# Eight W-high matmuls and then eight W-low ones in a chunk, in place of two and two

## The reference

```
for l in range(2):
    hn = rmsnorm(x, norm_mix[l])
    y  = even_mixer(hn, w_in, ..., w_out)  or  odd_mixer(hn, w_in, ..., w_out)
    x  = x + y
    h  = rmsnorm(x, norm_ffn[l])
    u  = causal_dwconv(h @ w_up, conv_w, conv_b)
    gate, val = split(u, 2)
    x  = x + (gelu(gate) * val) @ w_down
```

## Time and profile before

| | us |
|---|---|
| median of three runs | 2254.8 |
| the profiled execution's own time | 2255.13 |
| its span, first to last instruction | 2253.3 |
| TensorE busy (matmul) | 2245.3 (100%) |
| weight loads busy | 1954.4 (87%) |
| VectorE busy | 1543.9 (69%) |
| ScalarE busy | 1160.2 (51%) |
| mean granted TensorE clock | 1.000 |

### The profile page before, as it was taken

How to read it: one execution, slowest core, us unless ns; L and a number is a source line. 1 busy time by engine, 2 the same in 40 slices (tenths; PEclk the granted TensorE clock), 3 DMA queues, 4 the chain that set the end, 5 groups by cost and what they waited for, 6 DMA issues and landing times.

```text
span 2253.3 us, 34392 instructions
## 1 busy us (share of the span) xinstructions
PE 2245.3 (100%) x12726; PEld 1954.4 (87%) x12726; DVE 1543.9 (69%) x1753; ACT 1160.2 (51%) x1342; POOL 7.2 (0%) x17
## 2 busy tenths in 40 slices
PE   9999999999999999999999999999999999999999
PEld 8888888888888888888888888888888888888888
DVE  7886776777777777554577777667777777774444
ACT  6654355555555555444355555555555555553333
POOL 0000000000000000000000000000000000000000
PEclk9999999999999999999999999999999999999999
DMA  7555555666666656555665554556666666566664
GB/s 272 182 178 165 191 177 186 181 193 191 182 188 188 201 177 192 190 182 192 200 211 164 173 178 157 169 185 183 191 192 184 187 187 201 179 190 203 198 189 144
DMA packets 216387, 420.92 MB, mean 187 GB/s; under 512 B 13062, under 2 KB 13590, under 8 KB 216177
## 3 DMA queue, kind: packets, MB, share of 16 engines
q1 hardware_dynamic: 214416, 413.59, 58.8%
q0 software_dynamic: 1456, 5.65, 0.7%
q10 hardware_dynamic: 432, 0.56, 0.1%
HBM read 417.62 MB, written 2.12 MB: 186 GB/s over the span
## 4 chain that ended last, share of the span: by engine, by line
PE 99%; DVE 0%; DMA 0%; ACT 0%; issue 0%; ACTq 0%; DVEq 0%
PE ps L664 61%; PE ps L668 30%; PE ps L706 2%; PE ps L707 2%; PE ps L705 2%; PE ps L744 0%; PE ps L790 0%; PE ps L802 0%; PE ps L726 0%; DMA x_res<-x_t 0%; PE ps L745 0%; PE ps L738 0%; PE ps L801 0%; DVE aq L951 0%; PE ps L762 0%; ACT cross L377 0%
## 5 line engine op out<-in xcount | busy, mean ns | idle before, releaser
L943 DVE TENSOR_TENSOR w_lo<-raw,w_hi 128x1024 fp32r<-128x1024 f32 x783 | 948.5, 1223 | 497.3 <-ACT w_hi L369 477.5
L664 PE MATMUL ps<-xs,w_hi 128*128 128x512 f32 x3968 | 1248.3, 396 | 3.7 <-DVE w_lo L1379 3.4
L369 ACT ACTIVATE w_hi<-raw 128x1024 fp32r<-128x1024 f32 x783 | 811.3, 1055 | 560.1 <-PE ps L668 510.7
L668 PEld LDWEIGHTS ps<-xs,w_lo 128*128 128x128 f32 x3968 | 745.4, 188 | 176.1
L668 PE MATMUL ps<-xs,w_lo 128*128 128x256 f32 x3968 | 779.5, 278 | 0.0
L664 PEld LDWEIGHTS ps<-xs,w_hi 128*128 128x128 f32 x3968 | 605.0, 189 | 6.1 <-DVE xs L992 3.5
L664 PE MATMUL ps<-act,w_hi 128*128 128x512 f32 (+1 forms) x1912 | 600.7, 395 | 0.0
L668 PEld LDWEIGHTS ps<-act,w_lo 128*128 128x128 f32 x1912 | 359.2, 188 | 84.9
L668 PE MATMUL ps<-act,w_lo 128*128 128x256 f32 (+1 forms) x1912 | 375.6, 278 | 0.0
L664 PEld LDWEIGHTS ps<-act,w_hi 128*128 128x128 f32 x1912 | 291.1, 189 | 0.4 <-DVE av L968 0.4
L380 ACT ACTIVATE cross<-ps 128x1024 f32<-128x1024 f32 x72 | 74.0, 1027 | 119.5 <-PE ps L668 119.1
(11 more groups left out here) (186 smaller groups left out, 865.0 us busy)
## 6 DMA issues: line engine op xcount, KB each, us to landing
raw<-w_up SPq DMA_DIRECT2D x352, 512.0 KB, 3.7
raw<-w_in SPq DMA_DIRECT2D x191, 512.0 KB, 3.8
raw<-w_down SPq DMA_DIRECT2D x176, 512.0 KB, 4.6
raw<-w_out SPq DMA_DIRECT2D x64, 512.0 KB, 4.6
bias<-bias_line POOLq DMA_DIRECT2D x1, 2048.0 KB, 9.6
x_res<-x_t SPq DMA_DIRECT2D x3, 512.0 KB, 7.7
out_t<-x_res POOLq DMA_DIRECT2D x3, 512.0 KB, 3.1
gates_w<-w_gates POOLq DMA_DIRECT2D x1, 1024.0 KB, 5.4
```

The source lines that it names most:

```text
L369: act_f(w_hi[:, s, :, :], raw[:, s, :, :], ACT.Copy).then_inc(hi_ready, 1)
L664: return mm(ps[:, 4 * group + m, :], w_hi[:, s, u, m * P:(m + 1) * P], rhs, start=first and u == 0, stop=False)
L668: return mm(ps[:, 4 * group + m, 0:S], w_lo[:, s, u, m * P:(m + 1) * P], rhs[:, 0:S], start=False, stop=last and u == CT - 1)
L943: tt(w_lo[:, s, :, :], raw[:, s, :, :], w_hi[:, s, :, :].bitcast(F32), ALU.subtract).then_inc(lo_ready, 1)
```

## The change

Both K-tiles' moving operands are formed first. Then come the eight matmuls with W_hi (K-tile 0: output tiles 0 to 3, K-tile 1: output tiles 0 to 3), and then the eight with W_lo in the same order. The wait for the second half of a drained group stays ahead of the first matmul of output tile 2, which is now the third of the chunk, where it was the fifth. The first chunk's second wait stays ahead of the first matmul of K-tile 1, now the fifth, where it was the ninth. `chunk_values`, `last_chunk` and every other engine's program are unchanged.

```diff
+            rhs = [src[:, bass.ds(kt + u, 1), :, :].rearrange("p t a s -> p (t a s)") for u in range(CT)]
             for u in range(CT):
                 if tile_wait is not None and u == 1:
                     pe.wait_ge(lo_ready, 1)
-                rhs = src[:, bass.ds(kt + u, 1), :, :].rearrange("p t a s -> p (t a s)")
-
-                def hi(m):
-                    return mm(ps[:, 4 * group + m, :], w_hi[:, s, u, m * P:(m + 1) * P], rhs,
-                              start=first and u == 0, stop=False)
-
-                def lo(m):
-                    return mm(ps[:, 4 * group + m, 0:S], w_lo[:, s, u, m * P:(m + 1) * P], rhs[:, 0:S],
-                              start=False, stop=last and u == CT - 1)
-
-                for m in range(0, BT, 2):
+                for m in range(BT):
                     if drained is not None and (u, m) == (0, BT // 2):
 
                         pe.wait_ge(acc_drained, drained)
-                    hi(m)
-                    hi(m + 1)
-                    lo(m)
-                    ins = lo(m + 1)
+                    mm(ps[:, 4 * group + m, :], w_hi[:, s, u, m * P:(m + 1) * P], rhs[u], start=first and u == 0, stop=False)
+            for u in range(CT):
+                for m in range(BT):
+                    ins = mm(ps[:, 4 * group + m, 0:S], w_lo[:, s, u, m * P:(m + 1) * P], rhs[u][:, 0:S],
+                             start=False, stop=last and u == CT - 1)
             ins.then_inc(chunk_used, 1)
```

## The result

Eleven runs of the changed kernel have a median of 2261.03 us (2259.99 to 2262.69), eleven of the kernel before 2255.15 (2254.23 to 2256.15). The ratio is 1.0025, with a 95% interval of 1.0018 to 1.0033: slower by 5.9 us, 0.25%. The profiled execution of the changed kernel took 2261.78 us, 6.65 more than that of before; its span is 2260.0 us, 6.7 more. Of experiment 10's six runs one took 3200.78 us at a mean granted clock of 0.654; it is left out of that experiment's median and ratio.

The account below looks back on a forecast made before the run. TensorE's matmul pace was taken to bound the kernel. 2255.13 us + 4.7 for the chunks + 0.45 for the halved blocks = 2260.3, said as 2260 on the median's scale (+0.23%), range 2246 to 2266.

Parts of the forecast that it names:

- TensorE's pace is all that matters: Whole kernel: TensorE is busy 2245.3 of 2253.3 us, so the change acts on the time only through its pace.
- the ring's cover: ScalarE and VectorE feeding TensorE: four slots of 2.79 us cover their 2.3 us for a slot, so no cost.
- Hi run 1.840 us, lo run 0.9525, chunk +6.4 ns, +4.7 us: All 735 chunks: eight hi plus eight lo take 2.793 us against 2.787, adding 4.7 us.
- The dear beginning behind eight lo: Start of each hi run: the first six 512-column matmuls take 1.387 us, where the steady pace gives 1.360.
- Halved blocks +0.45 us, 0.15 each: Three halved blocks of layer 1: the third matmul's weight load waits for the drain; bounds 0 and 0.9 us.
- The first chunk at nothing: First chunk: its second wait comes at about 10.3 us, VectorE is done at 9.85, so no cost.
- the cheap way in: Rival, start of hi runs: five matmuls in 1.14 us, then steady; chunk 2.775 us, kernel 2247 us; chance 0.12.
- the quads' pace: Rival, lo runs: each lo keeps 0.115 us as in hi, hi, lo, lo groups; kernel 2236 us; chance 0.07.
- the exposed loads: Rival, lo runs: weight loads stretch the steps; 5 ns on seven gives 2286 us, bound 2605; chance 0.13.
- No change: Rival, all chunks: turning costs come out the same over a chunk, 2255 us; chance 0.12 including something between.
- T: Theory for the follow-ups: a matmul costs columns / 2.4 + 13.3 ns, each turn from lo to hi an extra.

Follow-up runs that it names:

- experiment 10: Changed kernel with 264-column lo matmuls, halved blocks' first chunks in the old order and 26 warm-up matmuls: 2246.16 us, ratio 0.9957 against the kernel before.
- experiment 6: Changed kernel, but the five chunks that start a halved block keep the old order (hi, hi, lo, lo): 2259.66 us in one profiled execution.
- experiment 7: Changed kernel with every chunk ordered six hi, six lo, two hi, two lo: 2251.91 us, ratio 0.9984 against the kernel before.
- experiment 3: Probe kernel with a different order of hi and lo matmuls in each stage, read by chunk times from one profiled execution; no kernel time given.
- 1,1: Probe stages with one hi and one lo matmul alternating, in place of eight and eight; the dearest order, expected 2770 to 2790 ns a chunk.
- 4,4: Changed kernel with four hi, four lo for each K-tile in place of eight and eight: 2269.29 us, ratio 1.0065 against the kernel before.
- 16 and 16: Changed kernel with odd chunks running lo first, so runs of sixteen form across chunks: 2253.85 us, ratio 0.9992 against the kernel before.
- 5,5,3,3: Probe stage with five hi, five lo, three hi, three lo in a chunk, in a down block of layer 0; no kernel time given.
- 6,6,2,2: Order of six hi, six lo, two hi, two lo: cheapest in the probe by stages; in the whole kernel 2251.91 us, ratio 0.9984 against before.

## Why the prediction was right

- *TensorE's pace is all that matters*: right. No other engine's busy time changed by more than 0.2 us, and the ring's cover held: ScalarE and VectorE show no wait that TensorE pays.
- *Hi run 1.840 us, lo run 0.9525, chunk +6.4 ns, +4.7 us*: right within 2 ns (1.842 and 0.952 measured). The steps that the kernel before shows where quads border on long runs came back one by one; the chunk is 2793.3 and not 2792.9, and the sum over the chunks of the order alone is 4.74 us. The dear beginning behind eight lo was the step that I argued for from a two-matmul sighting, and it held; with evidence that thin, a part of this is luck.
- *Halved blocks +0.45 us, 0.15 each*: 0.137 each, 0.41 in sum over the usual steps, shown by experiment 6. The wait is in the profile as that of the third weight load, 0.3 us long, of which 0.14 reach the pace.
- *The first chunk at nothing*: the wait cost nothing. But the clock's lower level there was neither foreseen nor in the sum. It costs 1.6 us in this profile, and by the medians of the runs with mean clocks of 1.000 and 0.999 1.1 us for the changed kernel and 1.3 for the one before. It accounts for the profile's 2261.78 against a sum of 2260.3.
- *The median*: 2260 said, 2261.03 measured with 2255.15 for before, +5.9 where I had +5.15. The order and the halved blocks account for 5.2. Among runs with a mean clock of 1.000 the difference is 5.5 (2260.09 against 2254.58), so part of the rest is the clock, which was at 1.000 in five of the changed kernel's eleven runs.
- *The rivals*: the cheap way in, the quads' pace and the exposed loads are not what happened, by the steps themselves. The cheap way in exists: in experiment 7 every run of six hi behind a pair of 116 and 113 starts with 232, 231, 227. Behind eight lo it doesn't come. The last rival has something to it, a floor of 112 ns, but it lies below what 256 columns take. "No change" is out as well: the ratio's interval, 1.0018 to 1.0033, doesn't hold 1, and the starts in the trace add up to the span.
- *What was wrong behind the right number*: the reason. "In quads the lo ones follow each other closely because each pair lives off the slack of two 512-column matmuls" explains none of experiment 3's ranking; 1,1 should then have been cheap. I had the right steps for this order and no general law, and the theory that I made of them (T) held for 4,4 and for 16 and 16 and failed for 1,1, for 5,5,3,3 and 6,6,2,2. Of the widths it gets the sum of the chunk, with 20 ns for the turn, within 4 ns at 240, 262, 272, 288 and 320 columns; at 264 and 268 it has 2820 and 2833 ns, where 2773.3 was measured, and at 224 and below it is too low. Why the steps are what they are, and why 264 columns are cheaper, stays open.

## What to carry to other kernels

Where TensorE is the bound and never waits, look for stretches in the old trace in which the new sequence of sizes already occurs, and add up their steps from start to start; that gave 6.4 ns in 2787 here. A count of turns or of hidden weight loads gives the wrong sign as easily as the right one. Order and width of alternating matmuls are worth a probe kernel that has another variant in each stage: it found 0.4% in one run, by a few columns *more*. And a wait that moves ahead by two matmuls costs even when the data come just in time: here the weight load of the third matmul waited for a drain that ended some 0.03 us before that matmul was due, and the block lost 0.14 us.

## What the hardware showed that was not expected

- The steady step of fp32r matmuls is columns / 2.4 + 13.3 ns at 256, 320 and 512 columns (120.0, 147, 226.7), but the mean step stays at 120 at 264 and 268 columns in the order 8,8. Alternation with 256 columns adds 7 to 53 ns to a chunk of sixteen, within 2 ns the same in every stage that has the same sequence. At the clock's lower level the steps are 427 and 213 ns, columns / 1.2 with nothing added.
- Eight lo matmuls of 264 columns behind eight hi are cheaper for the chunk than of 256, by 20 ns, and 268 are as cheap as 264; 262 and 266 are 40 dearer.
- Narrower than 248 columns next to nothing more is gained: 2733 ns at 248 and 224, 2720 at 192, 2747 at 128.
- After 1.7 to 3.6 us without matmuls at the start, the granted clock went to its lower level for 3.4 us or 6.8 us in five of ten profiles (the five had 2.3 to 2.9 us, but so had one of the other five), from between 0.6 us ahead of the first chunk's first matmul and 1.3 us behind it, and stayed at 1.00 in the other five.
